# Latent attention by pairs of heads, its constants loaded in pieces, Fourier and output weights split between other steps

## The chip, the core and the metric

The kernel runs on one core of a Trainium2 chip. The metric is device time in microseconds (us). Five engines work from programs of their own and meet at semaphores: TensorE (PE) multiplies, VectorE (DVE), ScalarE (ACT) and GpSimd (POOL) do the elementwise work, and SyncE (SP) issues the transfers from memory.

## The reference

Two blocks follow each other on one sequence of 512 tokens of width 1024. The first has two layers; its second layer, which the change touches, is this:

```python
f_in, f_gate, cq, ckv, kr, d_gate = _split_cd(h @ cd_w_in[j])
k_lat, v_lat = _mla_kv(ckv, kr, cd_kv_norm[j], cd_w_kv_up[j], rope)     # latent of width 128 -> 8 heads
q = _mla_q(cq, cd_q_norm[j], cd_w_q_up[j], rope)                        # latent of width 256 -> 8 heads of 64 + 32
attn = _block_attention(q, concat(k_ctx, k_lat), concat(v_ctx, v_lat))  # 512 queries, 768 keys, softmax
y = _cd_out(f_in, f_gate, attn, d_gate, cd_fnet_w[j], cd_w_out[j])      # Fourier mix beside attention, then one product
x = _post_norm(x, y, gt, cd_ln_g[j], cd_ln_b[j])
```

A head's query has 64 columns without position (NOPE) and 32 that are rotated (ROPE); the 32 rotated columns of the key are one set for all heads. The second block is a feed-forward, a mixing and a feed-forward step, twice. Everything is float32.

## The kernel before

Dense products are made of three products each: weights and activations are split in a high part (fp32r, a copy by ScalarE at L1403) and a low part (the rest, a subtraction by VectorE at L1809), and `mm3` adds hi·hi, hi·lo and lo·hi. Weights come in chunks of 1 MB through two buffers `raw`; chunk c is loaded when the low part of chunk c-2 is made (`raws_to`, L649). Each engine's program is written out in order: an instruction that waits holds all that stands behind it on its engine.

The layer runs so. `cd_in`: eight chunks, each two 512-column products of 24 matrix instructions; chunks 4 and 5 make the latents, which are turned to `cqT`, `ckvT` and `krT`. Then the Fourier product over features and over tokens, the product with `cd_fnet_w` (two chunks, 48 instructions), and the values of all heads (`vall`, six products). Attention is a loop of 32 steps, four blocks of 128 queries for each of 8 heads. In step n TensorE makes the scores of item n (two products, 512 and 256 columns), turns the probabilities of item n-1 (six transposes, L1164) and multiplies those of item n-2 with the values (24 small instructions). VectorE takes the row maximum of item n (L2180) and its scaled negative (L2182), copies a third of the turned probabilities of n-1 (L2189), and divides the product of n-2 (L2197). ScalarE makes the exponentials of n (L1635) and copies the other two thirds of n-1. Behind three of a head's four steps stand guests, the next head's keys, queries and rotation (`beside`, the dictionary at the loop's head): `head_keys` behind the first, `head_queries` behind the second, `head_rope` (one product with `rope_swap` and three passes of VectorE, L2146 to L2150) behind the third. Plain float32 products, all those of attention, are recorded as two instructions for each one.

After the loop the attention output is turned (L1184), gated and split for each of four token blocks, and `down` makes the output product: four weight chunks by four token blocks of 128 (`y`), 12 instructions for each pair of them. Chunk 0 of `cd_w_out` is split during the product with `cd_fnet_w`, chunks 1 to 3 behind the attention loop (`down`). A layer norm by VectorE, POOL and ScalarE follows each token block; its gain and bias rows (`cd_g`, `cd_b`) are loaded when the attention output is split, since they lie where `silu_dgate` was.

Of the kernel before, what the change touches and what calls it, by code (L numbers as in the profile page):

```python
# [8 lines left out]
F32 = mybir.dt.float32  # L9
# [5 lines left out]
P = 128  # L15
# [27 lines left out]
for _n, _k in VECS:  # L43
# [9 lines left out]
              (("C", 2), ((2176, P), (2560, P))), (("B", 1), ((1280, P), (1536, P))), (("A", 2), ((256, P), (640, P)))]  # L53
LATE_MOD = [("ab_w_mod", c0) for c0 in range(2 * D, 3 * D, CW)] + [("cd_w_mod", c0) for c0 in range(0, 3 * D, CW)]
# [262 lines left out]
def build(nc, A, out):  # L317
# [7 lines left out]
    with ctx:  # L325
# [33 lines left out]
        ln_put = signal("ln_put")  # L359
        mod_sum_made, silu_zeroed = signal("mod_sum_made"), signal("silu_zeroed")  # L360
# [32 lines left out]
        X = sb(ctx, "X", [P, NT, D])  # L393
        main_hi = sb(ctx, "h_hi", [P, KT, L], F32R)
# [14 lines left out]
        ctx_parts.close()  # L409
        wide = [sb(ctx, "wide", [P, D]) for _ in range(2)]  # L410
# [44 lines left out]
        q_up = sb(cd, "q_up", [P, 2, HEADS * QK])  # L455
        kv_up = sb(cd, "kv_up", [P, D])
        rope_c, rope_s = sb(cd, "rope_cos", [QK, L]), sb(cd, "rope_sin", [QK, L])
        swap = sb(cd, "rope_swap", [QK, QK])
# [10 lines left out]
        v_cols = kv_up[:, :].rearrange("p (h c) -> p h c", h=HEADS)[:, :, NOPE:P]
        kT_head = [None, None]  # L470
        qT_head = [None, None]
        for i in range(2):
            kT_head[i], qT_head[i] = sb(mla, "kT_head", [QK, LA]), sb(mla, "qT_head", [QK, L])
        probs = [sb(mla, "probs", [P, LA]) for _ in range(2)]
# [119 lines left out]
        work_order += [("gate_cd", 0), ("gate_cd", 1), ("rope", "kr")] + [("fnet", g) for g in range(4)] + [("rope", hd) for hd in range(HEADS)]  # L594
# [29 lines left out]
        def sync_program(sp):  # L624
# [88 lines left out]
            sp.dma_start(q_up[:, :, :], A["cd_w_q_up"][0].rearrange("(k p) n -> p k n", p=P)).then_inc(*mla_landed.mark("q_up"))  # L713
# [51 lines left out]
        def tensor_program(pe):  # L765
# [375 lines left out]
            for make in beside.values():  # L1141
                make(0)
# [1423 lines left out]
```

## Time and profile before

| | us |
|---|---|
| median of 3 runs | 2883.76 (2883.1 to 2891.36) |
| the profiled execution | 2889.03 |
| its span, first to last instruction | 2887.2 |
| TensorE busy | 2763.7 (96% of the span) |
| VectorE busy | 1162.8 (40%) |
| ScalarE busy | 957.7 (33%) |

The layer's part that the change touches lies between 386 and 720 us of the span. Times of the trace are counted from the span's start. The page gives the busy time of each engine, the chain of work that ended last, and groups of instructions; the timeline gives single instructions with the idle time before them and what ended it. A record may end a little after the next one starts.

### The profile page before, as it was taken

To read this page: it belongs to the slowest core of one execution; us is meant where nothing else is said; L and a number is where in the kernel's file an instruction comes from. 1 tells how busy PE (TensorE), PEld (TensorE's weight loads), DVE (VectorE), ACT (ScalarE), POOL (GpSimd) and SP (SyncE) were. 2 spreads that over 40 slices of the span, in tenths; PEclk is the share of its full clock that TensorE was granted. 3 is DMA by queue.
4 is the path that set the end of the run, shared out by engine and by line. 5 is a ranking of instruction groups with operands and counts; after the bars stand their busy time and mean duration, and the time that the engine had idled before them with its cause. 6 is when DMAs were issued, how large, how long until landed. Compare 5 with 4: busy or idle time off the path is not lost.

```text
span 2887.2 us, 34955 instructions
## 1 busy us (share of the span) xinstructions
PE 2763.7 (96%) x14803; PEld 2211.6 (77%) x14803; DVE 1162.8 (40%) x1735; ACT 957.7 (33%) x1429; POOL 143.7 (5%) x261
## 2 busy tenths in 40 slices
PE   7999999988999999997999999999999997999998
PEld 5887785557888887774788888888887774788887
DVE  3324652556333244446533324333243446533322
ACT  3222333442222234545322223222135445332221
POOL 0040000001000000001100000000001001100000
PEclk9999999999999999997999999999999997999999
DMA  9521231002332232110233222332232110223231
GB/s 304 186 99 36 82 123 44 1 11 86 103 102 90 100 109 58 58 44 30 74 102 102 90 100 102 102 99 92 102 96 69 59 45 30 73 95 99 91 102 73
DMA packets 208049, 250.06 MB, mean 87 GB/s; under 512 B 6400, under 2 KB 187223, under 8 KB 207895
## 3 DMA queue, kind: packets, MB, share of 16 engines
q1 hardware_dynamic: 207894, 247.83, 26.4%
q8 instruction: 118, 1.93, 0.3%
q14 instruction: 37, 0.30, 0.0%
HBM read 245.72 MB, written 2.10 MB: 86 GB/s over the span
## 4 chain that ended last, share of the span: by engine, by line
PE 88%; DVE 5%; ACT 3%; issue 2%; DMA 1%; POOL 1%; SPq 1%; DVEq 0%; POOLq 0%; ACTq 0%
PE psum L781 85%; PE psum L1243 1%; PE psum L1164 1%; PE psum L851 1%; DVE w_lo L1809 0%; ACT w_hi L1403 0%; DMA mod_w<-in_ab_w_mod 0%; DVE spare_lo L1809 0%; SPq L662 0%; DVE h_lo L1818 0%; ACT softplus L1761 0%; POOL stats_first L2412 0%; ACT softplus L1763 0%; DVE X L1881 0%; DVE stats_first L1885 0%
## 5 line engine op out<-in xcount | busy, mean ns | idle before, releaser
L781 PE MATMUL psum<-h_hi,w_hi 128*128 128x512 f32 (+1 forms) x2096 | 784.5, 374 | 6.6 <-ACT v_a L1412 4.1
L781 PE MATMUL psum<-h_lo,w_hi 128*128 128x512 f32 (+1 forms) x2096 | 778.7, 372 | 0.0
L781 PE MATMUL psum<-h_hi,w_lo 128*128 128x512 f32 (+1 forms) x2096 | 778.4, 371 | 0.0
L1809 DVE TENSOR_TENSOR w_lo<-raw,w_hi 128x2048 fp32r<-128x2048 f32 (+1 forms) x176 | 400.4, 2277 | 796.5 <-ACT w_hi L1403 796.2
L781 PEld LDWEIGHTS psum<-h_hi,w_hi 128*128 128x128 f32 x2096 | 398.1, 190 | 81.0 <-issue 14.7
L781 PEld LDWEIGHTS psum<-h_hi,w_lo 128*128 128x128 f32 x2096 | 397.6, 190 | 67.8
L781 PEld LDWEIGHTS psum<-h_lo,w_hi 128*128 128x128 f32 x2096 | 397.9, 190 | 65.7 <-issue 0.2
L1403 ACT ACTIVATE w_hi<-raw 128x2048 fp32r<-128x2048 f32 (+1 forms) x176 | 332.7, 1893 | 224.5 <-PE psum L781 217.8
L781 PE MATMUL psum<-w_hi,ff_hi 128*128 128x512 f32 x576 | 224.6, 390 | 0.0
L781 PE MATMUL psum<-w_lo,ff_hi 128*128 128x512 f32 x576 | 224.1, 389 | 0.0
L781 PE MATMUL psum<-w_hi,ff_lo 128*128 128x512 f32 x576 | 224.1, 389 | 0.0
L1412 ACT ACTIVATE work<-psum 128x512 f32<-128x512 f32 (+3 forms) x184 | 91.5, 503 | 398.6 <-PE psum L781 333.7
L781 PE MATMUL psum<-w_hi,h_hi 128*128 128x256 f32 (+2 forms) x512 | 167.8, 328 | 15.9 <-DVE w_lo L1809 13.9
L1679 ACT ACTIVATE ff_hi<-work 128x512 fp32r<-128x512 f32 (+1 forms) x96 | 57.3, 597 | 366.9 <-DVE work L2233 366.9
L781 PE MATMUL psum<-w_lo,h_hi 128*128 128x256 f32 (+2 forms) x512 | 161.6, 316 | 0.0
L781 PE MATMUL psum<-w_hi,h_lo 128*128 128x256 f32 (+2 forms) x512 | 161.4, 315 | 0.0
L2233 DVE TENSOR_TENSOR work<-work,psum 128x512 f32<-128x512 f32 (+1 forms) x96 | 61.7, 643 | 164.3 <-PE psum L781 164.2
L781 PEld LDWEIGHTS psum<-w_hi,ff_lo 128*128 128x128 f32 x576 | 108.2, 188 | 22.4
L781 PEld LDWEIGHTS psum<-w_lo,ff_hi 128*128 128x128 f32 x576 | 108.2, 188 | 22.3
L781 PEld LDWEIGHTS psum<-w_hi,ff_hi 128*128 128x128 f32 x576 | 108.1, 188 | 22.2
L781 PEld LDWEIGHTS psum<-w_hi,h_hi 128*128 128x128 f32 x512 | 100.9, 197 | 29.6 <-DVE w_lo L1809 14.6
L781 PEld LDWEIGHTS psum<-w_lo,h_hi 128*128 128x128 f32 x512 | 101.1, 197 | 4.7
(287 smaller groups left out, 3240.9 us busy)
## 6 DMA issues: line engine op xcount, KB each, us to landing
raw<-in_ffn_w_gate SPq DMA_DIRECT2D x44, 1024.0 KB, 5.3
raw<-in_ffn_w_up SPq DMA_DIRECT2D x44, 1024.0 KB, 5.3
raw<-in_ffn_w_down SPq DMA_DIRECT2D x44, 1024.0 KB, 4.8
raw<-in_w_in SPq DMA_DIRECT2D x36, 512.0 KB, 5.1
raw<-in_ab_w_in SPq DMA_DIRECT2D x10, 1024.0 KB, 7.7
mod_w<-in_ab_w_mod SPq DMA_DIRECT2D x8, 1024.0 KB, 11.8
raw<-in_w_out SPq DMA_DIRECT2D x8, 1024.0 KB, 4.8
raw<-in_cd_w_in SPq DMA_DIRECT2D x7, 1024.0 KB, 5.4
```

The source lines that it names most:

```text
L781: return pe.matmul(o, lhsT, rhs, start=start, stop=stop, skip_group_check=True)
L851: m = pe.transpose(bank(b, P, j * P), wide[1][:, k * P:(k + 1) * P], ident[:, :])
L1164: m = pe.transpose(bank(b + k // 4, P, (k % 4) * P), probs[(n - 1) % 2][:, k * P:(k + 1) * P], ident[:, :])
L1243: m = pe.transpose(bank(b, P, k * P), src[:, k * P:(k + 1) * P], ident[:, :])
L1403: act.activation(split_tiles(key)[0][:, 0:nk * n], raw[c % 2][:, 0:nk * n], ACT.Copy).then_inc(*w_hi_made.mark(key))
L1412: act.activation(o, src, func, **kw).then_inc(*kept.mark(name or event))
L1679: act.activation(ff_hi[:, k, off:off + n], work[used.index((k, half_)) % 3][:, 0:n], ACT.Copy).then_inc(*ff_hi_made.mark(event))
L1809: dve.tensor_tensor(lo[:, 0:nk * n], raw[c % 2][:, 0:nk * n], hi[:, 0:nk * n].bitcast(F32), ALU.subtract).then_inc(*w_lo_made.mark(key))
L2233: dve.tensor_tensor(w, w, full(event, n), ALU.mult).then_inc(*gated.mark(event))
```

## The change

Keys and queries are made for two heads at once: the weights are loaded in another order (`k_up`, `q_up_nope`: 64 columns for each head side by side), so a product of 128 output rows holds heads 2p and 2p+1, one in the upper and one in the lower 64 rows. The rotated columns of all queries are made ahead in two products (`qr`, four heads each) and rotated there, two rotations in place of eight; VectorE copies 32 rows of the result to each head's query (`pair_ropes`). Odd heads and slots contract over 128 rows, of which 32 are set to zero by POOL. The constants' loads have shorter rows: 32 floats for `q_up_rope`, 64 for `q_up_nope`, `k_up` and `v_up`. They are issued in groups around a `raw` chunk. The values and the first pair's keys and queries stand ahead of the product with `cd_fnet_w`, whose second chunk is split during the Fourier stage. The table of exponentials is loaded ahead of attention. All four chunks of `cd_w_out` are split in quarters of 512 columns inside the attention loop (`CD_PIECES`, behind 16 of the 32 steps), the SyncE queue loads them and the first two feed-forward chunks before it waits for the attention output, and the turning of that output stands behind the first part of the output product.

The diff, cut to its core, with eight columns of indentation left out:

```diff
@@ -51,6 +51,10 @@
+ROPE_AT, ZERO_AT = (2, 0, 3, 1), (None, 1, 2, 0)
+CD_PIECES = {n: divmod(i, 4) for i, n in enumerate((4, 6, 7, 8, 10, 12, 14, 15, 21, 22, 23, 24, 26, 27, 28, 30))}
@@ -710,12 +725,24 @@
-    sp.dma_start(q_up[:, :, :], A["cd_w_q_up"][0].rearrange("(k p) n -> p k n", p=P)).then_inc(*mla_landed.mark("q_up"))
-    sp.dma_start(kv_up[:, :], A["cd_w_kv_up"][0]).then_inc(*mla_landed.mark("kv_up"))
...
-    raws_to(CHUNK["cd", 0] + 2)
+    q_heads = A["cd_w_q_up"][0].rearrange("(k p) (h c) -> k p h c", p=P, c=QK)
+    kv_heads = A["cd_w_kv_up"][0].rearrange("p (h c) -> p h c", c=P)
+    sp.wait_ge(*swap_zeroed["all"])
+    for i in range(4):
+        if i == 2:
+            raws_to(CHUNK["cd_in", 0] + 6)
+        at = rows_of(i)
+        for k in range(2):
+            sp.dma_start(q_turn[:, k, :, ROPE_AT[i], :], q_heads[k][:, i::4, NOPE:QK]).then_inc(*mla_landed.mark("q_rope"))
+        sp.dma_start(rope_c[at, :], A["k_rope_cos"][NOPE:QK, :]).then_inc(*mla_landed.mark("rope"))
+        sp.dma_start(rope_s[at, :], A["k_rope_sin"][NOPE:QK, :]).then_inc(*mla_landed.mark("rope"))
+        sp.dma_start(swap[at, at], A["k_rope_swap"][NOPE:QK, NOPE:QK]).then_inc(*mla_landed.mark("rope"))
+    raws_to(CHUNK["cd_in", 0] + 6)
+    for k in range(2):
+        sp.dma_start(q_nope[:, k, :].rearrange("p (h c) -> p h c", c=NOPE), q_heads[k][:, :, 0:NOPE]).then_inc(*mla_landed.mark("q"))
+    sp.dma_start(k_up[:, :].rearrange("p (h c) -> p h c", c=NOPE), kv_heads[:, :, 0:NOPE]).then_inc(*mla_landed.mark("k"))
+    sp.dma_start(v_up[:, :].rearrange("p (h c) -> p h c", c=64), kv_heads[:, :, NOPE:P]).then_inc(*mla_landed.mark("all"))
+    raws_to(CHUNK["cd", 0] + 5)
@@ -881,6 +908,8 @@
                 m = down_part(s, nk, hi, lo, c, i, i * P, ready, chunks == TAIL and n == 0)
+                if s == "cd" and i == n == 0:
+                    attn_turns()
@@ -1080,11 +1109,16 @@
+    rope(("rope", "kr"), krT[:, 0:L])
+    for blk in range(2):
+        b = claim(rot.take(), ("qr", blk))
+        for k in range(2):
+            m = mm(bank(b), q_turn[:, k, blk, :, :].rearrange("p g c -> p (g c)"), cqT[:, k, :], k == 0, k == 1)
+        done(m, ("qr", blk))
@@ -1096,6 +1130,9 @@
+    for blk in range(2):
+        pe.wait_ge(*q_made["rope", blk])
+        rope(("rope", blk), q_rope[:, blk, :])
@@ -1105,6 +1142,24 @@
+    for t in range(6):
+        b = claim(rot.take(), ("vall", t))
+        done(mm(bank(b), ckvT[:, t * P:(t + 1) * P], v_up[:, :], True, True), ("vall", t))
+    def pair_keys(p):
+        for r, (off, n) in enumerate(RANGES):
+            b = claim(rot.take(), ("keys", p, r))
+            done(mm(bank(b, n), k_up[:, p * P:(p + 1) * P], ckvT[:, off:off + n], True, True), ("keys", p, r))
+    def pair_queries(p):
+        b = claim(rot.take(), ("queries", p))
+        for k in range(2):
+            m = mm(bank(b), q_nope[:, k, p * P:(p + 1) * P], cqT[:, k, :], k == 0, k == 1)
+        done(m, ("queries", p))
+    pair_keys(0)
+    pair_queries(0)
@@ -1147,11 +1179,16 @@
-                pe.wait_ge(*keys_shared[hd % 2])
-                pe.wait_ge(*rope_step["rope", hd])
+                pe.wait_ge(*q_made["head", hd])
+                pe.wait_ge(*q_turned[hd])
+                if hd < 4:
+                    pe.wait_ge(*keys_shared[hd])
+                if hd == 1:
+                    pe.wait_ge(*slots_zeroed["query", 3])
+            depth = P if hd % 4 else QK
...
-                m = mm(bank(b + r, width), qT_head[hd % 2][:, t * P:(t + 1) * P], kT_head[hd % 2][:, off:off + width], True, True)
+                m = mm(bank(b + r, width), qT[hd % 4][0:depth, t * P:(t + 1) * P], kT[hd % 4][0:depth, off:off + width], True, True)
@@ -1175,14 +1212,19 @@
+        if n < len(seq) - 8 and n % 8 == 1:
+            pair_keys(n // 8 + 1)
+        if n < len(seq) - 8 and n % 8 == 3:
+            pair_queries(n // 8 + 1)
+    def attn_turns():
+        pe.wait_ge(*attn_put["mla", HEADS - 1, NT - 1])
+        for t in range(NT):
+            b = claim(4 + t, ("attn", t))
+            for k in range(4):
+                m = pe.transpose(bank(b, P, k * P), o_mla[:, t, k * P:(k + 1) * P], ident[:, :])
+            done(m, ("attn", t))
@@ -1385,7 +1427,8 @@
-            act.wait_ge(*h_lo_made["attn", NT - 1])
+            act.wait_ge(*psum_full["queries", 3])
+            act.wait_ge(*rope_step["rope", 1])
@@ -1405,6 +1448,15 @@
+    def split_piece(c, i):
+        key = ("cd", c)
+        if i == 0:
+            act.wait_ge(*raw_landed[CHUNK[key] % 2][CHUNK[key]])
+            act.wait_ge(*psum_full["used", ("fnet", c)] if c < 2 else psum_full["queries", HEADS // 2 - 1])
+        at = slice(i * BANK, (i + 1) * BANK)
+        act.activation(split_tiles(key)[0][:, at], raw[CHUNK[key] % 2][:, at], ACT.Copy).then_inc(*w_hi_made.mark((key, i)))
@@ -1590,40 +1643,55 @@
+    for blk in range(2):
+        copy(q_rope[:, blk, :], ("qr", blk), full(("qr", blk)), q_made, ("rope", blk))
...
+        if hd == 0:
+            split_at(CHUNK["fnet", 1])
+        if hd == 1:
+            act.wait_ge(*rope_step["rope", "kr"])
+            for i in range(4):
+                at = rows_of(i)
+                act.activation(kT[i][at, :], krT[at, :], ACT.Copy).then_inc(*keys_shared.mark(i))
...
+    def pair_keys(p):
+        if p > 1:
+            act.wait_ge(*psum_full["scores", 2 * p - 3, NT - 1, 0])
...
+            event = ("keys", p, r)
+            for hd in (2 * p, 2 * p + 1):
+                p0 = 64 * (hd % 2)
+                copy(kT[hd % 4][p0:p0 + NOPE, off:off + n], event, rows(event, p0, p0 + NOPE, n), k_made, (hd, r))
...
+    def pair_queries(p):
...
+        for hd in (2 * p, 2 * p + 1):
+            p0 = 64 * (hd % 2)
+            copy(qT[hd % 4][p0:p0 + NOPE, :], event, rows(event, p0, p0 + NOPE), q_made, ("head", hd))
...
+    pair_keys(0)
+    pair_queries(0)
...
+    act.activation(stat("mla", 0, 2, 3), half[:, 0:1], ACT.Exp)
+    for g in range(3):
...
+    act.wait_ge(*psum_full["fnet", 3])
@@ -1641,8 +1709,14 @@
-        if n < len(seq) and seq[n][0] + 1 < HEADS and seq[n][1] in beside:
-            beside[seq[n][1]](seq[n][0] + 1)
+        if n < len(seq) - 8 and n % 8 == 1:
+            pair_keys(n // 8 + 1)
+        if n < len(seq) - 8 and n % 8 == 3:
+            pair_queries(n // 8 + 1)
+        if n == 0:
+            fnet_hi(3)
+        if n in CD_PIECES:
+            split_piece(*CD_PIECES[n])
@@ -1813,6 +1887,15 @@
+    def split_piece(c, i):
+        key = ("cd", c)
+        hi, lo = split_tiles(key)
+        at = slice(i * BANK, (i + 1) * BANK)
+        dve.wait_ge(*w_hi_made[key, i])
+        dve.tensor_tensor(lo[:, at], raw[CHUNK[key] % 2][:, at], hi[:, at].bitcast(F32),
+                          ALU.subtract).then_inc(*w_lo_made.mark(key if i == 3 else (key, i)))
@@ -2143,34 +2228,47 @@
+    rope(("rope", "kr"), krT[:, 0:L])
+    for blk in range(2):
+        rope(("rope", blk), q_rope[:, blk, :])
...
+        if hd == 0:
+            split_at(CHUNK["fnet", 1])
...
+    def pair_ropes(p):
+        if p > 1:
+            dve.wait_ge(*psum_full["scores", 2 * p - 3, NT - 1, 0])
+        for hd in (2 * p, 2 * p + 1):
+            at = rows_of(hd)
+            dve.tensor_copy(qT[hd % 4][at, :], q_rope[at, hd // 4, :]).then_inc(*q_turned.mark(hd))
+    dve.wait_ge(*rope_step["rope", 1])
+    pair_ropes(0)
...
+    for g in range(3):
@@ -2180,6 +2278,10 @@
+        if n == 0:
+            fnet_gate(3)
+        if n == 1:
+            fnet_lo(3)
@@ -2197,8 +2299,10 @@
+        if n < len(seq) - 8 and n % 8 == 5:
+            pair_ropes(n // 8 + 1)
+        if n in CD_PIECES:
+            split_piece(*CD_PIECES[n])
@@ -2442,10 +2546,24 @@
+    pool.wait_ge(*psum_full["y", "ab_c", NC - 1])
+    pool.memset(swap[:, :], 0.0).then_inc(*swap_zeroed.mark("all"))
...
+    pool.wait_ge(*psum_full["kv", 5])
+    pool.wait_ge(*rsqrt_made["kv", 5])
+    for i in range(1, 4):
+        if i > 1:
+            pool.wait_ge(*slots_zeroed["key", i - 1])
+        pool.memset(kT[i][32 * ZERO_AT[i]:32 * ZERO_AT[i] + 32, :], 0.0).then_inc(*slots_zeroed.mark(("key", i)))
+    pool.wait_ge(*psum_full["spec", 3])
+    for i in range(1, 4):
+        pool.wait_ge(*slots_zeroed[("query", i - 1) if i > 1 else ("key", 3)])
+        pool.memset(qT[i][32 * ZERO_AT[i]:32 * ZERO_AT[i] + 32, :], 0.0).then_inc(*slots_zeroed.mark(("query", i)))
+    pool.wait_ge(*slots_zeroed["query", 3])
```

What stands in a row on TensorE in a head's first two steps, before: `kT_head` and `qT_head` are a head's keys and queries, `probs` its probabilities.

```order
L781 MATMUL psum<-ckvT_63,kv_up_66 64x512
L781 MATMUL psum<-ckvT_63,kv_up_66 64x256
L781 MATMUL psum<-kT_head_79,qT_head_80 128x512
L781 MATMUL psum<-kT_head_79,qT_head_80 128x256
L1164 MATMUL psum<-ident_11,probs_81 128x128 x6
L781 MATMUL psum<-v_all_76,probsT_84 64x64 x12
L781 MATMUL psum<-cqT_62,q_up_65 96x512 x2
L781 MATMUL psum<-kT_head_79,qT_head_80 128x512
L781 MATMUL psum<-kT_head_79,qT_head_80 128x256
L1164 MATMUL psum<-ident_11,probs_82 128x128 x6
L781 MATMUL psum<-v_all_76,probsT_83 64x64 x12
L781 MATMUL psum<-qT_head_78,rope_swap_69 96x512
```

And now, in the third head's first step and on:

```order
L808 MATMUL psum<-v_all_90,probsT_92 64x64 x12
L808 MATMUL psum<-ckvT_71,k_up_75 128x512
L808 MATMUL psum<-ckvT_71,k_up_75 128x256
L808 MATMUL psum<-kT_26,qT_88 128x512
L808 MATMUL psum<-kT_26,qT_88 128x256
L1201 MATMUL psum<-ident_14,probs_10 128x128 x6
L808 MATMUL psum<-v_all_90,probsT_91 64x64 x12
L808 MATMUL psum<-kT_26,qT_88 128x512
L808 MATMUL psum<-kT_26,qT_88 128x256
L1201 MATMUL psum<-ident_14,probs_9 128x128 x6
L808 MATMUL psum<-v_all_90,probsT_92 64x64 x12
L808 MATMUL psum<-cqT_70,q_up_nope_73 128x512 x2
```

Keys and queries still stand behind scores, transposes and values, but come once in eight steps (behind steps 1 and 3 of a pair's eight), and no product with `rope_swap` stands in the loop.

On VectorE, before, the third and fourth step of a head:

```order
L2191 RECIPROCAL stats_first<-stats_first 128x1
L2197 TENSOR_SCALAR o_tok<-psum,stats_first 128x64
L2146 TENSOR_TENSOR work<-psum,rope_sin 96x512
L2148 TENSOR_TENSOR qT_head<-qT_head,rope_cos 96x512
L2150 TENSOR_TENSOR qT_head<-qT_head,work 96x512
L2180 TENSOR_REDUCE stats_first<-psum 128x1
L2182 TENSOR_SCALAR stats_first<-stats_first 128x1
L2189 COPY probsT<-psum 128x256
L2191 RECIPROCAL stats_first<-stats_first 128x1
L2197 TENSOR_SCALAR o_tok<-psum,stats_first 128x64
```

And now, behind steps 6 and 7:

```order
L1896 TENSOR_TENSOR w_lo<-raw,w_hi 128x512
L2278 TENSOR_REDUCE stats_first<-psum 128x1
L2280 TENSOR_SCALAR stats_first<-stats_first 128x1
L2291 COPY probsT<-psum 128x256
L2293 RECIPROCAL stats_first<-stats_first 128x1
L2299 TENSOR_SCALAR o_tok<-psum,stats_first 128x64
L1896 TENSOR_TENSOR w_lo<-raw,w_hi 128x512
L2278 TENSOR_REDUCE stats_first<-psum 128x1
L2280 TENSOR_SCALAR stats_first<-stats_first 128x1
L2291 COPY probsT<-psum 128x256
```

The three passes of the rotation are gone; a subtraction of 512 columns stands between the last work of a step and the next row maximum.

On TensorE at the end of attention, before:

```order
L1164 MATMUL psum<-ident,probs 128x128 x6
L781 MATMUL psum<-v_all,probsT 64x64 x24
L1184 MATMUL psum<-ident,o_tok 128x128 x16
L781 MATMUL psum<-w_hi,h_hi 128x512
L781 MATMUL psum<-w_lo,h_hi 128x512
L781 MATMUL psum<-w_hi,h_lo 128x512
```

And now:

```order
L808 MATMUL psum<-w_lo,h_hi 128x512
L808 MATMUL psum<-w_hi,h_lo 128x512
L808 MATMUL psum<-w_hi,h_hi 128x512
L808 MATMUL psum<-w_lo,h_hi 128x512
L808 MATMUL psum<-w_hi,h_lo 128x512
L1226 MATMUL psum<-ident,o_tok 128x128 x16
L808 MATMUL psum<-w_hi,h_hi 128x512
L808 MATMUL psum<-w_lo,h_hi 128x512
```

The turning (`o_tok`) has moved behind the first 12 of the output product's instructions, whose last five stand here.

## Rows read from the trace of the kernel before

**Rows 1.** Page, part 4: the chain that ended last, by engine.

```profile
PE 88%; DVE 5%; ACT 3%; issue 2%; DMA 1%; POOL 1%; SPq 1%; DVEq 0%; POOLq 0%; ACTq 0%
```

**Rows 2.** TensorE, before attention: start, us, line, work [idle before].

```profile
483.61 0.47 PE L781 MATMUL psum<-h_hi,w_hi 128*128 128x512 f32 x1 [1.46 <-issue]
...
494.57 5.31 PE L781 MATMUL psum<-kv_up,ckvT 128*128 128x512 f32 x12
...
504.96 1.10 PE L781 MATMUL psum<-qT_head,rope_swap 96*96 96x512 f32 x2 [1.75 <-ACT qT_head L1412]
508.43 2.90 PE L781 MATMUL psum<-kT_head,qT_head 96*128 96x512 f32 x4 [2.37 <-DVE qT_head L2150]
```

**Rows 3.** Stretch: busy us by engine, granted clock, DMA share, GB/s.

```profile
508.50:514.00 5.50, 5.50 (x9) 2.04 (x10) 1.11 (x2) 1.45 (x4) 0.00 (x0) 0.54 0.00 0
```

**Rows 4.** Chain by time, two heads' starts: start, us, what.

```profile
531.08 4.03 PE psum L781 x32
...
547.17 4.03 PE psum L781 x32
```

**Rows 5.** TensorE, keys, queries, rotation, one turning of probabilities.

```profile
607.92 1.46 PE L781 MATMUL psum<-ckvT,kv_up 128*64 128x512 f32 x4
...
612.30 1.96 PE L781 MATMUL psum<-cqT,q_up 128*96 128x512 f32 x4
...
616.99 1.10 PE L781 MATMUL psum<-qT_head,rope_swap 96*96 96x512 f32 x2
...
628.50 0.82 PE L1164 MATMUL psum<-ident,probs 128*128 128x128 f32 x6
```

**Rows 6.** VectorE, maxima of two bare steps.

```profile
625.71 0.96 DVE L2180 TENSOR_REDUCE stats_first<-psum 128x1 f32<-128x768 f32 x1 [1.12 <-PE psum L781]
...
628.70 0.96 DVE L2180 TENSOR_REDUCE stats_first<-psum 128x1 f32<-128x768 f32 x1 [1.12 <-PE psum L781]
```

**Rows 7.** ScalarE, the bare step between them.

```profile
626.95 0.90 ACT L1635 ACTIVATE probs<-psum,stats_first 128x768 f32<-128x768 f32 x1 [1.82 <-DVE stats_first L2182]
627.75 0.19 ACT L1635 ACTIVATION_READ_ACCUMULATOR probs<-psum,stats_first 128x1 f32 x1
627.84 0.59 ACT L1412 ACTIVATE probsT<-psum 128x512 f32<-128x512 f32 x1
```

**Rows 8.** ScalarE, a 512-wide high part.

```profile
638.56 0.63 ACT L1447 ACTIVATE h_hi<-work 128x512 fp32r<-128x512 f32 x1 [2.96 <-DVE work L2207]
```

**Rows 9.** VectorE: a 512-wide low part; layer norm's start and gain.

```profile
639.22 0.69 DVE L1818 TENSOR_TENSOR h_lo<-work,h_hi 128x512 fp32r<-128x512 f32 x1 [0.69 <-ACT h_hi L1447]
...
664.89 0.69 DVE L1878 TENSOR_TENSOR work<-psum,gate_rows 128x512 f32<-128x512 f32 x1 [4.87 <-PE psum L781]
...
669.32 1.28 DVE L1895 SCALAR_TENSOR_TENSOR X<-X,stats_first,g_row 128x1024 f32<-128x1024 f32 x1
```

**Rows 10.** TensorE, end of attention and output product.

```profile
634.85 1.78 PE L781 MATMUL psum<-v_all,probsT 128*64 128x64 f32 x48
637.08 1.97 PE L1184 MATMUL psum<-ident,o_tok 128*128 128x128 f32 x16 [0.45 <-DVE o_tok L2197]
...
649.34 0.80 PE L781 MATMUL psum<-w_hi,h_hi 128*128 128x512 f32 x1 [7.10 <-DVE w_lo L1809]
```

**Rows 11.** DMA issues: count, KB each, median us to landing.

```profile
b_row<-in_cd_ln_b SPq DMA_DIRECT2D x1, 512.0 KB, 5.2
...
lambda<-in_diff_lambda_q SPq DMA_DIRECT2D x4, 16.0 KB, 3.4
```

**Rows 12.** SyncE's queue: Fourier constants, bias row.

```profile
386.49 0.43 SPq L712 DMA_DIRECT2D dft_l<-in_k_dft_l  x1
...
646.30 0.43 SPq L721 DMA_DIRECT2D b_row<-in_cd_ln_b  x1
```

**Rows 13.** A stretch with the DMA engines full.

```profile
402.00:404.00 2.00, 2.00 (x19) 2.00 (x18) 0.64 (x3) 0.47 (x2) 0.55 (x1) 1.00 1.10 349
```

**Rows 14.** ScalarE, split of the last cd_in chunk.

```profile
423.25 1.91 ACT L1403 ACTIVATE w_hi<-raw 128x2048 fp32r<-128x2048 f32 x1
```

More of the change, by code:

```diff
@@ L393, in build @@
         X = sb(ctx, "X", [P, NT, D])
+        probs_scope = ExitStack()
+        sb(probs_scope, "first_blocks", [P, 4, L])
+        probs = [sb(probs_scope, "probs", [P, LA]) for _ in range(2)]
+        probs_scope.close()
         main_hi = sb(ctx, "h_hi", [P, KT, L], F32R)
@@ L409, in build @@
         ctx_parts.close()
+        keys_scope = ExitStack()
+        kT = [sb(keys_scope, "kT", [P, LA]) for _ in range(4)]
+        q_rope = sb(keys_scope, "q_rope", [P, 2, L])
+        keys_scope.close()
         wide = [sb(ctx, "wide", [P, D]) for _ in range(2)]
@@ L454, in build @@
         krT = sb(cd, "krT", [P, LA])
[L455 to L458, printed above, removed]
+        q_nope = sb(cd, "q_up_nope", [P, 2, HEADS * NOPE])
+        q_turn = sb(cd, "q_up_rope", [P, 2, 2, 4, ROPE])
+        k_up, v_up = sb(cd, "k_up", [P, HEADS * NOPE]), sb(cd, "v_up", [P, HEADS * 64])
+        rope_s, swap = sb(cd, "rope_sin", [P, L]), sb(cd, "rope_swap", [P, P])
+        f_in = sb(cd, "f_in", [P, 4, L])
+        rope_c = sb(cd, "rope_cos", [P, L])
+        dft_d = sb(cd, "dft_d", [P, 2 * P])
         fourier = ExitStack()
-        dft_d = sb(fourier, "dft_d", [P, 2 * P])
         dft_l = sb(fourier, "dft_l", [P, 4, 2, L])
-        f_in = sb(fourier, "f_in", [P, 4, L])
+        f_cs = [sb(fourier, "f_cs", [P, NT, 2 * P]) for _ in range(2)]
         silu_fg = sb(fourier, "silu_fgate", [P, 4, L])
-        f_cs = [sb(fourier, "f_cs", [P, NT, 2 * P]) for _ in range(2)]
         spec_hi, spec_lo = main_hi[:, 4:8, :], main_lo[:, 4:8, :]
@@ L467, in build @@
         mla = ExitStack()
+        qT = [sb(mla, "qT", [P, L]) for _ in range(4)]
         v_all = sb(mla, "v_all", [P, 6, HEADS * 64])
[L469 to L474, printed above, removed]
         probsT = [sb(mla, "probsT", [P, LA]) for _ in range(2)]
@@ L1057, in turn_kv @@
                 pe.transpose(bank(b, P), w[:, 0:P], ident[:, :])
-                done(pe.transpose(psum[0:QK, b * BANK + P:b * BANK + 2 * P], w[:, 64:160], ident[:, :]), ("kvt", t))
+                done(pe.transpose(bank(b, P, P), w[:, P:2 * P], ident[:, :]), ("kvt", t))
             pe.wait_ge(*h_lo_made["xo", NT - 1, 1])
```

105 lines of the change are left out of this document (31 added, 74 removed).

## The prediction

> **What bounds the kernel now.** I read the page's shares first, then the chain of waits. TensorE is busy 96% of the span and stands for 88% of the chain [rows 1]: the end moves by what leaves TensorE's program or its idle time, and by little else. Next the timeline of TensorE over 386 to 720 us, for its idle times. In the attention loop there is nearly none: a step without guest takes 2.99 us (the distance of two maxima, [rows 6]), filled with scores, turning and values. A head's period is 547.17 − 531.08 = 16.09 us [rows 4]; four bare steps are 11.96, so guests take 4.13 a head. Idle time stands in two places. Ahead of attention there are 1.46, 1.75 and 2.37 us [rows 2], and behind the last two the granted clock is 0.54, the lower level (1.2 GHz), in 508.5 to 514.0 [rows 3]. Behind attention TensorE waits 7.10 us for a low part of the output weights [rows 10].
>
> Last I asked how much room the other engines leave in a bare step. Maximum at 625.71, exponentials at 626.95 for 0.90 and their accumulator read to 627.94, copy of the turned probabilities 627.84 to 628.43 [rows 6, 7]. TensorE starts the next turning at 628.50 [rows 5] with no idle time; allowing some 0.15 from ScalarE's end to TensorE's start, the room is 628.50 − 627.94 − 0.15 = 0.41 us.
>
> **The loop.** Removed and added on TensorE: keys 1.46, queries 1.96, rotation 1.10 as recorded [rows 5], sum 4.52, of which 4.13 shows (records overlap), a factor 0.914: 1.33, 1.79 and 1.01. Before, guests stand in 7 heads: 7 × 4.13 = 28.9. Now keys and queries come for three pairs: 3 × (1.33 + 1.79) = 9.4 (a product with 128 output rows in place of 64 or 96 streams the same 512 columns, so I give it the same price; the bound above would be double, 9.4 more). Saved: 19.5.
>
> The lower clock: the row at 508.43 takes 2.90 for four score instructions [rows 2], where I estimate some 1.5 at the full clock by the size of the keys' row (1.46 for four, [rows 5]); over 508.5 to 514 at 0.54 of the clock, 5.5 × 0.46 = 2.5 us are lost. When the idle times ahead of it go, 2.6 come back, bounds 0 and 3. Against that, the loop now starts cold in another sense: its first turnings wait for the first maximum and exponentials, which no guest covers; 1.3 us of idle time by the chain maximum 0.96, exponentials 0.90, less a step's scores.
>
> The added work is the 16 quarter splits, a ScalarE copy of 512 columns (0.63, [rows 8]) and a VectorE subtraction of 512 (0.69, [rows 9]; some 0.61 behind another one). The subtraction stands in VectorE's program ahead of the next maximum, and it waits for ScalarE's copy, which stands behind exponentials and probability copy. So the pieces close a ring: maximum to exponentials 1.24, exponentials to copy 0.89 (627.84 − 626.95), copy to piece 0.50 to 0.59, high part 0.63, low part 0.61, then the next maximum: 1.24 + 0.89 + 0.53 + 0.63 + 0.61 = 3.90 against a step of 2.99. The first piece of a run eats the room: 0.91 − 0.41 = 0.50 of idle TensorE; each piece directly behind another costs 0.9. Steps with a guest have 1.3 to 1.8 of TensorE's work in them and swallow it. Going through the steps (4, 6, 7, 8, 10, 12, 14, 15, 21 to 24, 26 to 28, 30), with guests behind 9, 11, 17 and 19: seven first pieces cost, one of them with a longer tail (6 × 0.5 + 0.9 = 3.9), seven followers cost 0.9 (6.3), two (8→9 and 10→11) nothing. Sum 10.2, with 0 and 16 × 0.9 = 14.4 as bounds. This is the term I trust least, and the middle is what the rows give. `pair_ropes` (two VectorE copies of 32 × 512) stands in bare steps; at the price of the low part or less it is about 1.2 us beside VectorE's own idle time of 1.12 [rows 6] and some more behind it, free; if uncovered three times 0.5. POOL's zeroing lies on an engine that is idle.
>
> Loop: 19.5 + 2.6 − 1.3 − 10.2 = 10.6 saved.
>
> **Ahead of the loop.** Idle 1.46 + 1.75 + 2.37 = 5.6 go, and one rotation for head 0 (0.9): 6.5. They go because values, keys and queries now stand between, because the exponentials' table is loaded earlier, and since the rotation's chain of ScalarE and VectorE runs before the Fourier stage. Added are the two `qr` products (four recorded instructions each, as the queries: 2 × 1.79 = 3.6) and two rotations (2 × 0.9): 5.4. Saved: 1.1; bounds −4 (the idle time comes back elsewhere) and 3.
>
> **The tail.** Before, attention ends on TensorE at 634.85 + 1.78 = 636.63, and the first token block's product is done at about 664.75, where VectorE's layer norm starts [rows 9, 10]: 28.1 us. Its work is 48 instructions; 48 such take 494.57 − 483.61 = 10.96 between the Fourier rows [rows 2], and the turning takes 1.97 [rows 10], so 12.8 as placed now. The rest was split chains: 7.10 of wait, the shorter ones after it, and the lower clock they bring. With all four chunks split in the loop nothing is late but the gated output of attention, and the turning stands behind 12 instructions (2.7 us), which covers the 0.45 of wait ahead of it. Saved: 15.3. What is late next: the bias row. Both rows are still issued when attention's output is split (before at 646.30, [rows 12], 9.7 behind attention's end); now I put that at 11.6 behind its end, as split and product share the engines. 512 KB land 5.2 us after the issue [rows 11], so the bias at 17.2; VectorE needs the gain at 12.8 + 4.4 (669.32 − 664.89) and the bias after 1.28 more. Cost 0 to 0.4, I take 0.2. From there on layer norm by token block (some 13.5 us each) goes its old way, shifted. Saved: 15.1, bounds 12 and 16.
>
> **Small transfers.** `q_up_rope` comes in 4 × 2 × 128 × 2 = 2048 packets of 128 B, `q_up_nope`, `k_up` and `v_up` in 4096 of 256 B; 5120 of them, 320 for each of 16 DMA engines, stand ahead of `cd_in`'s last chunk. The rows have such packets only in a tiny load (below). A full packet of 1 KB takes 47 ns (349 GB/s over 16 engines, [rows 13]); at that price they take 15 us where their bytes took 4, and the chunk, landed at some 405 before, lands at 416 to 418. Its split starts at 423.25 [rows 14], and TensorE meets it only if it lands after about 430: free up to 85 ns a packet. Upper bound: the lambda load, 16 KB in single small rows, takes 3.4 us from issue to landing [rows 11]; eight packets to an engine are at most 425 ns each, most of it fixed latency. I take 47 ns, the nearest row, so 0.
>
> The stretch with the engines full moves 349 GB/s in 1 KB packets [rows 13]. The Trainium skill, "DMA: Bandwidth & Descriptors", section "Why small descriptors are slow (HBM only)", says that a packet carries fixed overhead on the bus and 32 bytes of descriptor data; it puts the first at 27% for 256 B, an estimate by which such packets cost a few ns more than their bytes and less than my 47, and the sum stays. It speaks against the change all the same, since the same bytes came in longer rows before; no row here shows by how much.
>
> **Sum.** 10.6 + 1.1 + 15.1 = 26.8 us. The profiled execution took 2889.03 (its span 2887.2 and 1.8 around it) and would take 2862.2. It lies 5.3 above the median of the runs; off the median, 2883.76 − 26.8 = 2857.0.
>
> **Rivals.**
> A. The pieces hide wholly: 2857 − 10.2 = 2846.8. For it: VectorE and ScalarE are busy 40% and 33% of the span. Against: the ring is a chain, not a load, and 3.90 exceeds 2.99.
> B. The clock falls in the piece runs of steps 21 to 30. For it: short idle times of 1.75 and 2.37 were enough for 0.54 [rows 2, 3]. Against: mine are 0.5 to 0.9, and between them TensorE works. Ten steps of 2.99 at about 0.6 of the clock cost some 20 us: 2876. The Trainium skill, "TensorE: Matmul & The Clock Gate", section "A second HAM failure mode: psum-queue depth-cycling", describes a clock that oscillates when an engine with much work idles often and briefly; by it this rival holds, and the trace agrees only as far as rows 3.
> C. The small packets are late: at 190 ns each, 320 × (190 − 85) = 34 us of TensorE waiting for `cd_in`'s last chunk, which takes the gain and more: 2857 + 34 = 2891. It decides from 85 + 26.8 / 320, some 170 ns a packet (nothing left of the gain). For it: the lambda load's bound of 425. Against: that is latency of one transfer.
> D. Fewer guests bring nothing, since the ring of VectorE and ScalarE then sets every step's period; only the tail and the start are saved, 15.1 + 1.1 = 16.2: 2867.6. For it: a room of only 0.41 [rows 5 to 7]. Against: bare steps already run at TensorE's pace.
>
> **How the numbers follow.** Forecast as above 0.66 (2850 to 2864 by the bounds of pieces and clock), A 0.12, B 0.08, C 0.04, D 0.10. The range 2846 to 2870 holds the forecast's own range, D, and half of A, 0.82 of the chance. A measurement of this kernel tells about 0.3% (8.65 us) from no change. Faster by over that, under 2875.1: the forecast, A and D, 0.88. Within: B, whose 2876 lies just above that bound, 0.08. Slower: C, 0.04.
>
> **What would show it.** Right: no `rope_swap` row in the loop; eight steps take 23.9 plus 3.1 plus the stalls; TensorE's turnings behind piece steps show 0.5 and 0.9 of idle time ended by ScalarE's `probs` or VectorE; the granted clock is 1.00 over 500 to 700 but for the loop's start; no wait for `w_lo` near the 7.10; the first layer-norm row 12.8 us behind the last values; the last chunk of `cd_in` landed before VectorE and ScalarE come to it. Wrong: turnings behind guest-free piece steps without idle time (A); 0.5 of the clock in the runs of pieces (B); TensorE waiting at 425 to 430 for `w_hi` of `cd_in` (C); bare steps without a piece above 2.99 (D). A product of 128 output rows that costs double would show in the rows of keys and queries.

## The result, and the profile after

| | before | after |
|---|---|---|
| median of 4 runs, us | 2887.56 (2883.1 to 2896.43) | 2862.14 (2861.4 to 2864.26) |
| the profiled execution's span | 2887.2 | 2860.7 |
| TensorE busy | 2763.7 | 2744.6 |

The ratio is 0.9909, with a 95% interval of 0.9882 to 0.9937. Forecast were 2857 us and 26.8 us saved; saved are 25.4 by the medians and 26.5 by the two spans.

The whole time of one kernel scatters by several us from run to run, and with it the mean granted clock (one kernel below took 2839.3 us at 0.979 and 2852.4 at 0.973). Stages inside the changed layer scatter far less: where an edit didn't touch them, those from the first load to the fourth block's turning repeated within 0.05 us in the nine further profiles of changed kernels, and within 0.25 in a second one of the kernel before. So the saving is read stage by stage, from starts of single rows (all in us; "turning" is TensorE's transposing, "last values" the last product of probabilities with the values):

| stage | before | after | saved |
|---|---|---|---|
| start to the Fourier constants' first load | 386.11 | 387.09 | −0.98 |
| to the first scores | 122.32 | 120.23 | 2.09 |
| to the last step's maximum | 123.26 | 110.97 | 12.29 |
| to the end of the last values | 4.94 | 4.92 | 0.02 |
| to the first layer norm row | 28.26 | 13.18 | 15.08 |
| to the fourth block's turning | 54.69 | 54.67 | 0.02 |
| to the feed-forward's first low part | 12.01 | 14.02 | −2.01 |
| to the end | 2155.61 | 2155.62 | 0 |

The forecast had 1.1, 10.6 and 15.1 for the three stages that it spoke of, 26.8 in all; they saved 29.5. The two losses, of 0.98 and 2.01, make it 26.5; they are looked at below.

The timeline of TensorE in the loop (start, us, line, work, and in brackets the idle time before it and what ended it):

```profile
535.17 0.85 PE L1201 MATMUL psum<-ident,probs 128*128 128x128 f32 x6 [0.38 <-ACT probs L1703]
...
539.04 0.85 PE L1201 MATMUL psum<-ident,probs 128*128 128x128 f32 x6 [0.69 <-ACT probs L1703]
539.81 0.92 PE L808 MATMUL psum<-v_all,probsT 128*64 128x64 f32 x24
540.66 1.56 PE L808 MATMUL psum<-ckvT,k_up 128*128 128x512 f32 x4
542.82 1.56 PE L808 MATMUL psum<-kT,qT 128*128 128x512 f32 x4 [0.60 <-ACT probs L1703]
```

The same kernel, a pair's queries (its own two products, four records):

```profile
577.56 1.99 PE L808 MATMUL psum<-cqT,q_up_nope 128*128 128x512 f32 x4
```

Keys and queries of two heads take what those of one took (1.56 and 1.99, against 1.46 and 1.96 in [rows 5]): 128 output rows cost no more than 64 or 96. Nor do more rows to contract over: scores over 128 rows take 1.45 to 1.56, those over 96 take 1.46 to 1.56. From turning to turning, a piece step takes 539.04 − 535.17 = 3.87 us, against 2.99 for a bare one [rows 6]. The idle time (0.69) is less than the 0.88 that the step is longer: where nothing waits, the turning's row starts 0.17 before the scores' row ends (scores at 516.06 for 1.56, turning at 517.45), and a wait takes that overlap away too.

VectorE in the same stretch:

```profile
536.06 0.69 DVE L1896 TENSOR_TENSOR w_lo<-raw,w_hi 128x512 fp32r<-128x512 f32 x1 [1.52 <-ACT w_hi L1459]
536.67 0.95 DVE L2278 TENSOR_REDUCE stats_first<-psum 128x1 f32<-128x768 f32 x1
```

VectorE waits 1.52 us for ScalarE's high part with the next maximum queued behind it. And the chain of waits, in a run of pieces, is on ScalarE and VectorE (start, duration, what):

```profile
594.32 0.53 ACT spare_hi L1459
594.85 0.02 issue
594.87 0.69 DVE spare_lo L1896
595.57 0.88 DVE stats_first L2278
```

At the end of attention the wait of 7.10 [rows 10] is gone, and with it a second one of the kernel before, for the low part of the next weight chunk:

```profile
660.08 0.64 PE L781 MATMUL psum<-spare_hi,h_hi 128*128 128x512 f32 x1 [3.06 <-DVE spare_lo L1809]
```

Now layer norm starts 13.18 us behind the last values (TensorE's row first, then two of VectorE):

```profile
621.43 1.78 PE L808 MATMUL psum<-v_all,probsT 128*64 128x64 f32 x48
...
626.73 0.69 DVE L2311 TENSOR_TENSOR work<-psum,silu_dgate 128x512 f32<-128x512 f32 x1 [3.12 <-PE psum L1226]
...
636.39 0.69 DVE L1961 TENSOR_TENSOR work<-psum,gate_rows 128x512 f32<-128x512 f32 x1 [1.62 <-PE psum L808]
```

TensorE is busy for 13.00 of the 13.00 us from 623 to 636. The granted clock stands at 1.00 through the loop, also where before it was 0.54 [rows 3] (columns as there):

```profile
508.00:516.00 8.00, 6.88 (x51) 4.50 (x49) 5.12 (x11) 4.91 (x11) 0.00 (x0) 1.00 0.00 0
516.00:630.00 114.00, 106.51 (x1104) 74.03 (x1099) 66.91 (x177) 61.51 (x123) 0.00 (x0) 1.00 0.12 38
```

### The profile page after: what moved, and what is told of

Its sections match the earlier page's. It is cut to its first block, busy times and chain, and to the rows that moved or that the text cites. A ratio compares the mean times of both kernels' runs of the same rounds, so it can differ in the third digit from the quotient of the medians.

```text
span 2860.7 us, 34916 instructions
## 1 busy us (share of the span) xinstructions
PE 2744.6 (96%) x14767; PEld 2208.0 (77%) x14767; DVE 1153.9 (40%) x1737; ACT 963.0 (34%) x1446; POOL 147.2 (5%) x268
## 4 chain that ended last, share of the span: by engine, by line
PE 87%; DVE 6%; ACT 3%; issue 2%; DMA 1%; POOL 1%; SPq 1%; DVEq 0%; ACTq 0%; POOLq 0%
PE psum L808 84%; PE psum L1285 1%; PE psum L878 1%; DVE stats_first L2278 1%; DMA mod_w<-in_ab_w_mod 0%; DVE w_lo L1883 0%; SPq L677 0%; ACT w_hi L1446 0%; DVE spare_lo L1883 0%; DVE h_lo L1901 0%; ACT softplus L1835 0%; POOL stats_first L2516 0%; ACT softplus L1837 0%; PE psum L1201 0%; DVE X L1964 0%
## 5 line engine op out<-in xcount | busy, mean ns | idle before, releaser
L808 PEld LDWEIGHTS psum<-w_hi,h_hi 128*128 128x128 f32 x512 | 100.5, 196 | 19.5 <-issue 5.6
L808 PEld LDWEIGHTS psum<-w_hi,h_lo 128*128 128x128 f32 x512 | 100.1, 196 | 5.4
```

Of the source, the lines that this page charges most:

```text
L808: return pe.matmul(o, lhsT, rhs, start=start, stop=stop, skip_group_check=True)
```

## The experiments

All start from the changed kernel, but for two that have the late low parts of the first experiment as well and for one that is the kernel before. Their stages are compared with the table above. The median of the kernel before beside these runs was 2889.7 to 2891.4, and of each stage there is one profile for each kernel.

**Low parts one step later.** On VectorE, `split_piece` moves from the end of a step to behind the next step's maximum and its scaled negative:

```diff
+                if n - 1 in CD_PIECES:
+                    split_piece(*CD_PIECES[n - 1])
...
-                if n in CD_PIECES:
-                    split_piece(*CD_PIECES[n])
```

> The low part of a piece stands one step later, behind that step's maximum and its scaled negative; the high part stays. Theory (ring of maximum, exponentials, copy, high part, low part, next maximum sets 3.87 us for a piece step against 2.99): the ring is open, idle time ahead of the turnings behind piece steps goes, the loop is 8 to 9.5 us shorter, about 2853 us. Rival (ScalarE's copy of 0.63 delays the exponentials, or the tiles' ports are busy): steps stay at 3.87 and the time within 2 us of the changed kernel.

First scores to last maximum: 101.81 in place of 110.97, so 9.2 us less, and no other stage from the first load to the fourth block's turning moves by over 0.03. The median is 2848.64, the ratio to before 0.9857 (0.9836 to 0.9878). VectorE now:

```profile
534.58 0.96 DVE L2278 TENSOR_REDUCE stats_first<-psum 128x1 f32<-128x768 f32 x1 [0.66 <-PE psum L808]
535.57 0.15 DVE L2280 TENSOR_SCALAR stats_first<-stats_first 128x1 f32<-128x1 f32 x1
535.64 0.68 DVE L1896 TENSOR_TENSOR w_lo<-raw,w_hi 128x512 fp32r<-128x512 f32 x1
...
537.57 0.96 DVE L2278 TENSOR_REDUCE stats_first<-psum 128x1 f32<-128x768 f32 x1 [0.66 <-PE psum L808]
```

The high part has long been made when the low part comes, so it waits for nothing, and the step is 537.57 − 534.58 = 2.99 again. From turning to turning so is every step without a guest but the last. The same 16 high and 16 low parts are done: their work is free and their order cost 9.2 us. ScalarE's share stayed where it was, so the rival falls.

Step by step, from turning to turning, the changed kernel takes longer than this one by 0.42 to 0.54 for pieces 4, 6, 12, 14, 21 and 27 (numbers are those of the steps), by 0.88 for 7, 15, 22, 23, 24 and 28, by 0.89 for 8, and by nothing for 10, 26 and 30; 0.1 more stands behind the runs. Two of these need a word. TensorE idles 0.91 us ahead of the last turning, but it does so in every kernel, this one and the kernel before included:

```profile
634.07 0.84 PE L1164 MATMUL psum<-ident,probs 128*128 128x128 f32 x6 [0.91 <-ACT probs L1635]
```

And piece 8 isn't hidden by the keys made behind step 9: the next scores (at 542.82 above) still wait for item 9's exponentials, which end at 541.77 + 0.90 = 542.67:

```profile
541.77 0.90 ACT L1703 ACTIVATE probs<-psum,stats_first 128x768 f32<-128x768 f32 x1 [1.87 <-DVE stats_first L2280]
```

By the kernel's text that is a matter of result banks: `rot` gives the eight of them out in turn, and behind the keys' two the scores of item 10 get those of item 9. The queries take one, and piece 10, with queries behind step 11, cost nothing. No run moved the banks.

**All pieces behind the loop,** on ScalarE and on VectorE:

```diff
-                if n in CD_PIECES:
-                    split_piece(*CD_PIECES[n])
+                if n == len(seq) + 1:
+                    for i in range(16):
+                        split_piece(*divmod(i, 4))
```

> All 16 quarter splits stand behind the attention loop on ScalarE and VectorE, none in it. Theory: the loop is some 9.5 us shorter (no piece steps); the tail from the last values to the first layer norm row grows from 13.2 to about 21 to 23 us, since 16 low parts of 0.69 and a load of chunks 2 and 3 of 5 us each stand in it before the output product can end. Net -1 to +2 us against the changed kernel, so the pieces in the loop as placed bought nearly nothing. Rival (the loop's stalls come from elsewhere, from the copies for pairs of heads): loop unchanged, net +8 to +10 us.

The loop is 101.81, to 0.01 the same as with late low parts: nothing is left in it of the pieces there, nor here. Steps without a guest take 2.99 here too, so the copies for pairs of heads cost nothing. The tail is 25.14 in place of 13.18, 2 to 4 us worse than expected. TensorE waits for the low parts of the weights, and then for the attention output's split, which stands behind all 16 pieces:

```profile
618.89 0.50 PE L808 MATMUL psum<-w_hi,h_hi 128*128 128x512 f32 x1 [3.20 <-DVE w_lo L1897]
632.08 0.76 PE L808 MATMUL psum<-spare_hi,h_hi 128*128 128x512 f32 x1 [5.67 <-DVE h_lo L1902]
```

So the pieces as placed by the change brought 11.96 in the tail and cost 9.16 in the loop, net 2.8 us. The medians (2859.73, of runs from 2848.5 to 2866.8, and 2862.14) don't separate the two kernels; the stages do.

**Guests doubled.** `mm` of keys and queries of pairs 1 to 3 stands twice:

```diff
+                    if p:
+                        mm(bank(b, n), k_up[:, p * P:(p + 1) * P], ckvT[:, off:off + n], True, True)
...
-                for k in range(2):
+                for k in range(4 if p else 2):
+                    k = k % 2
```

> Every product of the keys and queries of pairs 1 to 3 is made twice; nothing else. Theory (TensorE sets the loop, a pair's keys and queries cost 3.12 us): +9.4 us less what hides stalls behind guest steps, 8 to 9.5 us. Rival D (the chain of VectorE and ScalarE sets every step, guests are free): 0 to +3 us.

The loop grows from 110.97 to 119.14, by 8.17, within the theory's range (median 2866.65). A doubled pair of queries:

```profile
521.13 3.70 PE L808 MATMUL psum<-cqT,q_up_nope 128*128 128x512 f32 x8
```

From turning to turning, each of the three doubled queries adds 1.72, and the doubled keys add 1.29, 0.43 and 1.29. So a pair's keys and queries cost 3.01 us, and only the keys behind step 9 fill a wait, of 0.86. TensorE's work in the loop counts nearly in full, and rival D falls.

**Products to keep the clock up, in three tries.** The stretch ahead of the feed-forward was 2.0 us longer after. Its row, and the stretch's clock:

```profile
691.06 1.94 PE L878 MATMUL psum<-ident,wide 128*128 128x128 f32 x8 [5.39 <-DVE wide L1994]
```

```profile
688.00:690.00 2.00, 0.00 (x0) 0.00 (x0) 0.37 (x1) 0.96 (x3) 0.74 (x2) 0.60 0.00 0
690.00:692.00 2.00, 0.94 (x5) 0.97 (x6) 0.92 (x1) 0.00 (x0) 0.00 (x0) 0.50 0.00 0
```

First try, 36 products right behind the fourth block's last output product:

```diff
+                            if s == "cd" and i == NT - 1:
+                                b = claim(rot.take(), ("warm", s))
+                                for k in range(36):
+                                    mm(bank(b, P), ident[:, :], ident[:, :], True, True)
```

> 36 products of the identity with itself, 128 columns, without a reader, stand behind the fourth token block's output product, where TensorE is idle for 6 us ahead of the feed-forward. Theory (the 2.0 us given back behind the layer norm are the lower clock over 688 to 695, which follows that idle time): granted clock 1.00 there, 1 to 2 us less than the changed kernel. Rival (the lower clock comes from the products' own lighter load at 672 to 678, or the loss is something else): same time, dip stays.

A miss by placement: there the third block's turning is still to come, and it waited behind 8.20 us of products. The stage to the fourth block's turning grew from 54.67 to 58.16, and 3.87 us of idle time stayed behind it, with the clock at the lower level after it (0.50 over 696 to 698). Median 2865.62.

Second try, on the kernel with late low parts: 20 of these behind `follow(i - 1)`, so behind the third block's turning.

> The late low parts, and 20 products of the identity with itself (4.6 us, no reader) behind the turning of the third token block, where TensorE is idle for 5.2 us; in the earlier try they stood ahead of that turning and held it up. If idle time ahead of the feed-forward makes the lower clock there: the stretch from the fourth block's turning to the feed-forward's first low part goes from 13.6 to about 12.0 us, and the whole lies 1.6 below the kernel with late low parts alone. If not: stretch 13.6 as before.

Stretch 13.58, against 13.61 without them, and median 2848.54 against 2848.64. Of the idle time 2.27 us were left, and the clock still fell:

```profile
682.44 1.94 PE L878 MATMUL psum<-ident,wide 128*128 128x128 f32 x8 [2.27 <-DVE wide L1998]
```

Third, 28 of them:

> Late low parts, and 28 products in place of 20 ahead of the fourth block's turning: TensorE's idle time of 2.27 us there shrinks to about 0.4. If idle time right ahead of the feed-forward brings the lower clock: the stretch to the first low part falls from 13.6 to 12.0 us. If it stays near 13.6, the idle time there is not its cause (an earlier one is).

Now 0.48 us of idle time is left, the clock is 1.00 over 660 to 688, and the stretch is 12.11:

```profile
684.11 1.06 PE L878 MATMUL psum<-ident,wide 128*128 128x128 f32 x8 [0.48 <-DVE wide L1998]
```

The median of this kernel is 2842.35 (2839.95 to 2848.9), ratio 0.9842 (0.9816 to 0.9867), the lowest of all run here; against 2848.64 without the products the ranges overlap. Only the stage's 1.5 us are shown, and by one profile: the kernel before has one too in which the clock doesn't fall there, with nothing added, as the next run tells.

**The kernel before, once more.**

> The kernel before, once more, for a second profile: which stages repeat and which don't. If the stretch from the fourth block's turning to the feed-forward's first low part (12.01 before, 14.02 after) belongs to the change, it is 12.0 again; if the clock's low phase falls there by chance, it lies anywhere between 12 and 14. The stages from 386 us to the first layer norm row repeat within 0.1 us.

The same stretch is 14.37 us here, with the clock at 0.50 over 720 to 724:

```profile
719.42 1.94 PE L851 MATMUL psum<-ident,wide 128*128 128x128 f32 x8 [5.40 <-DVE wide L1911]
```

```profile
720.00:724.00 4.00, 4.00 (x21) 4.00 (x20) 2.14 (x4) 1.61 (x3) 0.00 (x0) 0.50 0.01 4
```

So the 2.01 us that the changed kernel seemed to give back aren't its own: the stretch is about 12.0 where the lower clock misses it and 13.3 to 14.4 where it meets it, whichever the kernel. The first profile of the kernel before had its lower clock earlier, behind the third block's turning:

```profile
706.00:708.00 2.00, 2.00 (x11) 2.00 (x10) 2.00 (x3) 0.00 (x0) 0.00 (x0) 0.50 0.70 190
```

There it cost nothing, since TensorE had to wait for the fourth block in any case: the idle time ahead of it was 2.68 us in place of 5.40, and the stage to it 54.69 against 54.67. The other stages of the second profile are 122.37, 123.14, 4.93 and 28.51; they differ from the first profile's by up to 0.25 (the last), where 0.1 was expected. The first stage differs too between kernels that don't differ there (385.4 to 389.3 in all profiles).

**Rows of 64 B.** `q_up_nope`, `k_up` and `v_up` come in four loads of 16 columns a head each:

```diff
+            for f in range(0, NOPE, 16):
+                sp.dma_start(k_up[:, :].rearrange("p (h c) -> p h c", c=NOPE)[:, :, f:f + 16], kv_heads[:, :, f:f + 16]).then_inc(*mla_landed.mark("k"))
```

> The 4096 rows of 256 B (q_up_nope, k_up, v_up) are loaded as 16384 rows of 64 B, by 16 instructions in place of 4; 1024 packets for each DMA engine in place of 256, ahead of cd_in's last chunk. At some 27 ns a packet (what the changed kernel's trace suggests for its 384 packets and 6.5 us more of full engines) the chunk lands near 434 and TensorE loses 0 to 5 us; at the 47 ns of the prediction it lands near 454 and TensorE loses about 20 us. If transfers of constants were wholly beside the path at any size: 0.

Nothing moved: 120.22 to the first scores, every stage behind that within 0.05, median 2862.76. The profile counts 12,480 more packets under 512 B than in the changed kernel, and the stretch full of 64 B packets reads (columns as in rows 13):

```profile
408.00:412.00 4.00, 4.00 (x38) 4.00 (x38) 3.34 (x5) 1.44 (x3) 0.54 (x2) 1.00 0.91 85
```

85 GB/s over 16 engines are 64 × 16 / 85 = 12 ns for a packet of 64 B. Loads of 256 B rows in the changed kernel moved 200 GB/s over 403 to 405, some 20 ns each. Both are far under the 47 of the prediction, which was itself far from the 85 at which TensorE would have noticed. The DMA engines move nothing over 422 to 426, so `cd_in`'s last chunk has landed by 422, where 434 or later was expected. ScalarE starts its split at 424.86, against 424.35 in the changed kernel, whose first load is 0.52 earlier: on time in both.

**No early table.** `act.activation(stat("mla", 0, 2, 3), half[:, 0:1], ACT.Exp)` is left out.

> The one-column exponential ahead of attention, which loads ScalarE's table early, is left out. If the table matters: the first exponentials come some 1.3 us later and TensorE's idle time of 1.12 in the loop's first steps grows to about 2.4, so +1.3 us from the first maximum on. Rival (ScalarE waits long enough, or the table's load is no longer than the wait for the first maximum): 0.

First scores to last maximum: 112.25, so +1.28. The load stands ahead of the first exponentials, and TensorE's idle time is 2.40 there in place of 1.12:

```profile
508.38 1.28 ACT L1702 ACT_TABLE_LOAD   x1 [3.81 <-DVE stats_first L2279]
...
510.82 0.84 PE L1201 MATMUL psum<-ident,probs 128*128 128x128 f32 x6 [2.40 <-ACT probs L1702]
```

The median of two runs is 2858.44, lower than the changed kernel's 2862.14: the 1.28 us is seen in the stage and lost in the scatter of the whole. The early load isn't a gain over the kernel before, it keeps the other gains whole: there the load came at 504.92, in the wait for the first head's rotation, and ScalarE then still waited 6.34 us for the first maximum.

**Turning first.** `attn_turns()` stands ahead of `down` again.

> The turning of the attention output stands ahead of the output product again, as before the change; pieces as in the changed kernel. Theory: TensorE waits 0.4 to 0.9 us for the last attention output there (0.45 before), nothing behind it waits less, so 13.18 becomes 13.6 to 14.1 us. Rival (the gated split of the first token block is what ends the tail, and an earlier turning makes it ready sooner): 13.18 or a little less.

13.61 in place of 13.18: +0.43, by the wait of 0.45 that is back (median 2864.98, which doesn't show so little):

```profile
622.21 1.97 PE L1224 MATMUL psum<-ident,o_tok 128*128 128x128 f32 x16 [0.45 <-DVE o_tok L2298]
```

## Why the prediction was right

Guests and clock in the loop. With the pieces out of the way the loop takes 101.81 against 123.26, so 21.45 us less; the terms 19.5 + 2.6 − 1.3 make 20.8. By the doubled guests, three pairs cost 3 × 3.01 = 9.0, not 9.4, so the guests saved 28.9 − 9.0 = 19.9. The other 1.6, forecast as 1.3, are the clock less the idle time at the loop's start: before, the first scores and keys took 5.36 us (508.43 to 513.79), where by the rows at full clock two such take some 2.7, so 2.7 came back, less an idle time of 1.12. Same price for 64 and 128 output rows: held. The clock at the loop's start is 1.00, and the idle time ahead of it is gone, as said; no run put that idle time back alone.

Pieces. The ring of 3.90 us against 2.99 was right to 0.03 (3.87), and so was the price of a first piece in a step (0.42 to 0.54 where 0.50 was taken) and of a follower (0.88 where 0.9 was taken). The sum of 10.2 was 1.0 too high, measured 9.2, because of which pieces pay. Piece 30, by its place the one "with a longer tail" that was given 0.9, costs nothing: the idle time there is in the kernel before too, which could have been read beforehand. The run 26 to 28 costs 0.9 less than taken (26 nothing, 27 as a first piece); why is open. Against that, piece 8 costs 0.89 where a guest was to hide it. That the term was the one "trusted least" was fair; that the forecast didn't ask what else the pieces' place could be is what it lacked: 9.2 us stood there to be taken.

Ahead of the loop 2.1 were saved where 1.1 was taken. The two traces tell where. Up to the end of the Fourier product the added products and rotations cost 5.2 (5.4 taken), and the rotation of `krT` starts 0.1 later. From there to the first scores 26.3 us became 18.9, 7.4 less where 6.5 was taken: the three waits cost more than their 5.6 of idle time, since each also takes away an overlap of some 0.17 between rows, 0.5 in all; some 0.3 is not placed. The early table, which the prediction names among the reasons, has no part in it: its load cost nothing before, and its 1.28 would have come behind this stage, in the loop's first steps.

Tail. 15.08 against 15.1. The parts: 11.96 from the splits being done in time, rather than behind the loop all at once, 0.43 from the turning's place, 2.7 from the rest. Read from the traces, TensorE idled 10.7 us of this stage before (0.45, 0.13, 7.10 and 3.06) and not at all now. Of the other 4.3 some 3.7 are the lower clock that came with it before, an estimate from TensorE's busy 2.66, 4.00 and 4.92 us at 0.50, 0.82 and 0.66 (648 to 652, 652 to 656, 660 to 665). The forecast's work for the new tail is a little small (10.96 + 1.97 is 12.9 and not 12.8; measured 13.18). The bias row was not late: its operation at 642.64 waits 0.52 for POOL's statistics, as before, so the 0.2 put on it was nothing.

Small transfers. Free, as taken, but by a margin much wider than argued; rival C needed 170 ns and 64 B packets take 12. The bound of 425 from one tiny load held that load's whole latency and was no price of a packet; it should have held no chance.

Rival A (pieces hide) was false for this order and true for another. B (the clock falls in piece runs) is false: 1.00 over 516 to 630 with 14 idle times of 0.25 to 0.91. D is false.

The sum. That 26.8 met 26.5 is in part luck. The three stages saved 29.5, 2.7 more than forecast (1.7 in the loop, 1.0 ahead of it), and two stages that the change doesn't touch happened to take 3.0 more in the one profile than in the other. The medians of the kernel before beside the experiments, of seven runs each, are 2889.7 to 2891.4; against them the change saves 27.6 to 29.3. The median came 5 us above the forecast mainly because that was made from a before-median of 2883.76 of three runs; with four it was 2887.56.

## What to carry to other kernels

An engine at 40% can still cost the bound engine 0.9 us a step: price an inserted instruction by what it waits for and by what is queued behind it, as a ring over the engines, not by its own length. When such a ring closes, try the inserted half one step later, where its input has long been made. A wait costs its idle time and the overlap of rows that it takes away. Where whole times scatter by more than an effect, compare stages between fixed rows of the traces, and profile the kernel before twice, to see which stage differences belong to the change.

## What had not been expected of the hardware

Packets of 64 B cost 12 ns on a DMA engine and those of 256 B some 20 ns, while a packet of 1 KB takes 47. Idle times of 0.25 to 0.91 us in a row left the granted clock at 1.00. An idle time of 2.68 us ahead of the fourth block's turning left it at 1.00 in one profile of the kernel before (first row below; the stretch in the second), while 2.27 in the kernel with 20 products was followed by the lower level, so the length of the last idle time alone doesn't tell whether it falls. What differs ahead of it: in the first the clock had been at 0.50 up to some 8 us before, in the second it was at 1.00 from 20 to 2 us before. Three of the ten profiles of changed kernels show the clock low twice, some 10 to 15 us before this turning and at it; the slower products then fill part of the idle time, 3.9 us of it are left in place of 5.4.

```profile
719.58 1.06 PE L851 MATMUL psum<-ident,wide 128*128 128x128 f32 x8 [2.68 <-DVE wide L1911]
```

```profile
718.00:720.00 2.00, 0.42 (x4) 0.45 (x5) 1.28 (x1) 0.00 (x0) 0.11 (x1) 1.00 0.00 0
720.00:722.00 2.00, 2.00 (x19) 2.00 (x18) 1.13 (x2) 1.09 (x2) 0.00 (x0) 1.00 0.00 0
```
